# A seven-product FFN: the four weight sums of a column pair moved from GpSimd arithmetic to accumulating DMAs, and a second plain column pair ahead of the products

## The reference

```
def swiglu(x, w_gate, w_up, w_down):
    return (jax.nn.silu(x @ w_gate) * (x @ w_up)) @ w_down
...
hdn = rmsnorm(x, gains[0])
x = x + 0.5 * rmsnorm(swiglu(hdn, ffn_w_gate[layer, 0], ffn_w_up[layer, 0], ffn_w_down[layer, 0]), gains[1])
```

## Time and profile before

| | |
|---|---|
| median of 3 runs | 2672.76 us |
| the profiled execution | 2667.47 us, span 2665.7 us |
| PE busy | 2488.1 us, 93% of the span, mean granted clock 0.974 |
| DVE, ACT, POOL busy | 1749.6, 1096.3, 1009.2 us |
| seven-product phases (first to last matmul, us from the span's start) | 67 to 293, 942 to 1168, 1355 to 1581, 2283 to 2509 |
| moved by DMA | 264 MB, mean 99 GB/s |

### The profile page before, as it was taken

One profiled execution on the slowest core, in us unless ns is written; L12 is line 12 of the kernel. 1 busy time (PEld: TensorE's weight loads), 2 busy tenths in 40 slices (PEclk: granted clock), 3 DMA queues, 4 the chain that ended last, 5 costly groups with the idle time before them and its releaser, 6 DMA issues. The chain is left out here.

```text
span 2665.7 us, 50729 instructions
## 1 busy us (share of the span) xinstructions
PE 2488.1 (93%) x19573; PEld 2346.5 (88%) x19573; DVE 1749.6 (66%) x2614; ACT 1096.3 (41%) x2074; POOL 1009.2 (38%) x937
## 2 busy tenths in 40 slices
PE   5999999998999879999969999999999989699998
PEld 5899999995557879999969999999979969699998
DVE  6998525546664699862599882467546566998723
ACT  3554424114443445442445452334344444454422
POOL 3556103023331365620265630165245533656201
PEclk8999999999999989999989999999999999899999
DMA  3233432348894123343123343223210133133431
GB/s 98 80 96 96 121 85 65 80 129 286 301 306 151 48 64 96 96 120 90 29 79 96 96 124 87 64 65 88 65 34 2 33 105 92 50 95 107 112 87 45
DMA packets 315918, 264.16 MB, mean 99 GB/s; under 512 B 10984, under 2 KB 288693, under 8 KB 315688
## 3 DMA queue, kind: packets, MB, share of 16 engines
q1 hardware_dynamic: 304176, 223.03, 28.4%
q0 software_dynamic: 11536, 38.28, 4.3%
HBM read 251.71 MB, written 9.56 MB: 98 GB/s over the span
## 5 line engine op out<-in xcount | busy, mean ns | idle before, releaser
L750 PE MATMUL ps<-x_part_hi,part_hi 128*128 128x272 f32 x2240 | 660.6, 295 | 90.6 <-DVE part_lo L795 70.4
L750 PE MATMUL ps<-x_part_hi,part_lo 128*128 128x272 f32 x2240 | 654.0, 292 | 0.0
L750 PE MATMUL ps<-x_part_lo,part_hi 128*128 128x272 f32 x2240 | 650.7, 290 | 0.0
L506 DVE TENSOR_TENSOR w_lo<-w_raw,w_hi 128x1024 fp32r<-128x1024 f32 (+1 forms) x154 | 225.8, 1466 | 493.4 <-ACT w_hi L499 488.0
L750 PEld LDWEIGHTS ps<-x_part_hi,part_hi 128*128 128x128 f32 x2240 | 427.5, 191 | 103.0 <-DVE part_lo L795 72.4
L499 ACT CAST w_hi<-w_raw 128x1024 fp32r<-128x1024 f32 (+1 forms) x154 | 182.1, 1182 | 605.1 <-PE ps L534 546.0
L750 PEld LDWEIGHTS ps<-x_part_lo,part_hi 128*128 128x128 f32 x2240 | 428.5, 191 | 0.0
L750 PEld LDWEIGHTS ps<-x_part_hi,part_lo 128*128 128x128 f32 x2240 | 427.5, 191 | 0.0
L795 DVE TENSOR_TENSOR part_lo<-w_pair,part_hi 128x512 fp32r<-128x512 f32 x320 | 329.7, 1031 | 45.4 <-ACT part_hi L788 43.4
L1381 POOL TENSOR_TENSOR xT<-xT,rstd_rows 128x272 f32<-128x272 f32 x96 | 84.4, 909 | 696.5 <-DVE rstd_rows L1406 696.5
L795 DVE TENSOR_TENSOR part_lo<-w_sums,part_hi 128x512 fp32r<-128x512 f32 x240 | 260.7, 1086 | 20.0 <-ACT part_hi L788 19.3
(11 more groups left out here) (565 smaller groups left out, 5031.3 us busy)
## 6 DMA issues: line engine op xcount, KB each, us to landing
...
v_pages<-in_cache_a_v_dram POOLq DMA_DIRECT2D x128, 256.0 KB, 4.5
...
```

The source lines that it names most:

```text
L506: e.tensor_tensor(w_lo[:, n % 2, 0:nk * P], raw[:, n % RAW, 0:nk * P], w_hi[:, n % 2, 0:nk * P].bitcast(F32), ALU.subtract).then_inc(sem(" ...
L750: mm = e.matmul(ps[:, bank, 0:TH], w[:, k * P:(k + 1) * P], x[:, k, :], start=idx < 4 and k == 0 and w is wh and x is xp_hi[idx], stop=k = ...
```

## The change

The second pair of columns of gate and up is done plainly too (`STD` = 2), so that eight plain units run ahead of 18 pairs (`WP` = 18) with 126 products. The ring has four slots, not five, in four of its 26 rounds, so that 126 parts end at the same slot as 140 did.

The scheme's signs are turned so that all four sums of weights are plain sums: t3 = b12 + b22, t2 = b11 + t3, b12 + b11, t2 + b21. Some activation quarters are scaled by a negated gain (`minus_gains`) instead, and `dve_sums` subtracts where it added. Each sum is a DMA from SBUF to SBUF, issued from POOL's queue, which adds its source to its destination. A sum that may not overwrite an operand needs it twice: SP loads b12's quarter (4 x 128 rows) and b11's once more into `w_sums`. A pair is loaded by four DMAs of 512 + 256 + 512 + 256 KB, where it was two of 512 KB. The buffer's layout is now tile by tile, so that a row of a load is 512 bytes, where it was 1 KB.

POOL does no arithmetic in the gate and up phase. Its four sums of activations are DVE's, between the splits of the seventh and the eighth plain unit. For the first two pairs SP waits for the raw slots that lie under the buffer (`raw_free`).

```
-HP = KF // 2 - 1
-WP = 2 * HP
+STD = 2
+WP = 2 * (KF // 2 - STD)
 LATE = 10
+DMA_SUMS = ("t2", "t4")
...
-        w_pair = [place(f"w_pair_{x}", [P, KD, 2 * P], F32, at=at_w + x * 12288)[0] for x in range(2)]
+        w_pair = [place(f"w_pair_{x}", [P, 2, KD, P], F32, at=at_w + x * 12288)[0] for x in range(2)]
...
-                gemm(f"gate_up{l}{w}", "gate_up", 1, KD, gate_up)
+                gemm(f"gate_up{l}{w}", "gate_up", STD, KD, gate_up)
...
+        SLOTS = [(c, s) for c in range(KF + 4) for s in range(RING - short(c))]
...
-            return (w_pair[x][:, 0:KH, 0:P], part_rows(w_sums[x][:, 1, :]), w_pair[x][:, 0:KH, P:2 * P],
-                    part_rows(w_sums[x][:, 0, :]), w_pair[x][:, KH:KD, 0:P], w_pair[x][:, KH:KD, P:2 * P],
+            return (w_pair[x][:, 0, 0:KH, :], part_rows(w_sums[x][:, 1, :]), w_pair[x][:, 1, 0:KH, :],
+                    part_rows(w_sums[x][:, 0, :]), w_pair[x][:, 0, KH:KD, :], w_pair[x][:, 1, KH:KD, :],
                     part_rows(w_sums[x][:, 1, :]))[idx]
...
         def sp_gate_up(e, g, down):
             f = ffn_of(g)
             l, w = int(g["name"][-2]), int(g["name"][-1])
+            for i in range(STD):
+                for j in range(4):
+                    sp_unit(e, g, i, j)
+            of = (rows(io["ffn_w_gate"][l, w]), rows(io["ffn_w_up"][l, w]))
+
+            def raw_free(slot):
+                e.wait_ge(sem("w_lo_ready"), g["first"] + 4 * (STD - 1) + (slot - g["first"]) % RAW + 1)
+
+            for p in range(WP):
+                x, at = home(g, p), (STD + p // 2) * 2 * P
+                m1, m2 = slice(at, at + P), slice(at + P, at + 2 * P)
+                if p >= 2:
+                    wait_step(e, "vector", f, "part", PROD * (p - 1) - 1)
+                if p < 2:
+                    raw_free(2 * x + 1)
+                e.dma_start(w_pair[x][:, 1, :, :], of[p % 2][:, :, m2]).then_inc(sem(f"w_pair{p % 2}"), 16)
+                if p < 2 and x:
+                    e.wait_ge(sem("unit_done"), g["first"] + 4 * STD - 1 + (1 if g["first"] % 2 else 0))
+                e.dma_start(part_rows(w_sums[x][:, 0, :]), of[p % 2][:, 0:KH, m2]).then_inc(sem(f"w_pair{p % 2}"), 16)
+                if p < 2:
+                    raw_free(2 * x)
+                e.dma_start(w_pair[x][:, 0, :, :], of[p % 2][:, :, m1]).then_inc(sem(f"w_pair{p % 2}"), 16)
+                if p < 2 and x:
+                    e.wait_ge(sem("unit_done"), g["first"] + 4 * STD - 1 + (1 if g["first"] % 2 else 0))
+                if p < 2 and not x:
+                    raw_free(2)
+                e.dma_start(part_rows(w_sums[x][:, 1, :]), of[p % 2][:, 0:KH, m1]).then_inc(sem(f"w_pair{p % 2}"), 16)
             for j in range(4):
-                sp_unit(e, g, 0, j)
-            of = (rows(io["ffn_w_gate"][l, w]), rows(io["ffn_w_up"][l, w]))
-            for p in range(WP):
-                if p < 2:
-                    e.wait_ge(sem("w_lo_ready"), g["first"] + 4)
-                else:
-                    wait_step(e, "vector", f, "part", PROD * (p - 1) - 1)
-                at = (1 + p // 2) * 2 * P
-                for x in range(2):
-                    k = slice(x * KH, (x + 1) * KH)
-                    e.dma_start(w_pair[p % 2][:, k, :], of[p % 2][:, k, at:at + 2 * P]).then_inc(sem(f"w_pair{p % 2}"), 16)
-            for j in range(4):
-                wait_step(e, "vector", f, "part", PROD * (WP - (1 if (down["first"] + j) % RAW < 2 else 0)) - 1)
+                slot = (down["first"] + j) % RAW
+                early = slot in ((0, 1) if home(g, WP - 1) else (3,))
+                wait_step(e, "vector", f, "part", PROD * (WP - early) - 1)
                 sp_unit(e, down, 0, j)
...
+        W_LOADS = 4
+
         def pair_landed(e, f, p):
-            e.wait_ge(sem(f"w_pair{p % 2}"), 32 * ((WP * f + p) // 2 + 1))
+            e.wait_ge(sem(f"w_pair{p % 2}"), 16 * W_LOADS * ((WP * f + p) // 2 + 1))
+
+        W_ADDS = 4
+
+        def added(e, f, p, n):
+            e.wait_ge(sem(f"w_added{p % 2}"), 16 * (W_ADDS * ((WP * f + p) // 2) + n))
 
         def pool_gate_up(e, g):
             f = ffn_of(g)
-
-            for n, (to, a, b, op) in enumerate(((2, 3, 6, ALU.add), (1, 2, 0, ALU.subtract), (3, 0, 3, ALU.subtract),
-                                                (5, 4, 1, ALU.subtract))):
-                wait_step(e, "vector", f, "xn", (7, 11, 11, 15)[n])
-                if n:
-                    wait_step(e, "gpsimd", f, "x_sum", n - 1)
-                e.tensor_tensor(x_sums[:, to, :, :], x_sums[:, a, :, :], x_sums[:, b, :, :],
-                                op).then_inc(sem("ffn_gpsimd"), did("gpsimd", "x_sum", n))
             for p in range(WP):
-                x = p % 2
-                if p == 1:
-                    e.wait_ge(sem("unit_done"), g["first"] + 4)
+                x = home(g, p)
                 pair_landed(e, f, p)
-                b11, b12, b21, b22 = (w_pair[x][:, k:k + KH, m:m + P] for k in (0, KH) for m in (0, P))
+                b11, b21, b12, b22 = (w_pair[x][:, c, k:k + KH, :] for c in range(2) for k in (0, KH))
                 t3, t2 = (part_rows(w_sums[x][:, y, :]) for y in range(2))
-                e.tensor_tensor(t3, b22, b12, ALU.subtract).then_inc(sem("ffn_gpsimd"), did("gpsimd", "w_sum", 4 * p))
-                wait_step(e, "gpsimd", f, "w_sum", 4 * p)
-                e.tensor_tensor(t2, t3, b11, ALU.add).then_inc(sem("ffn_gpsimd"), did("gpsimd", "w_sum", 4 * p + 1))
-                e.tensor_tensor(b12, b12, b11, ALU.subtract).then_inc(sem("ffn_gpsimd"), did("gpsimd", "w_sum", 4 * p + 2))
-                wait_step(e, "gpsimd", f, "w_sum", 4 * p + 1)
+                e.dma_start(t3, b22, accum_op=ALU.add).then_inc(sem(f"w_added{p % 2}"), 16)
+                e.dma_start(b12, b11, accum_op=ALU.add).then_inc(sem(f"w_added{p % 2}"), 16)
+                added(e, f, p, 2)
+                e.dma_start(t2, t3, accum_op=ALU.add).then_inc(sem(f"w_added{p % 2}"), 16)
                 wait_step(e, "vector", f, "part", PROD * p + 1)
-                e.tensor_tensor(t2, b21, t2, ALU.subtract).then_inc(sem("ffn_gpsimd"), did("gpsimd", "w_sum", 4 * p + 3))
-
+                added(e, f, p, 3)
+                e.dma_start(t2, b21, accum_op=ALU.add).then_inc(sem(f"w_added{p % 2}"), 16)
...
+            if idx in (1, 2, 3, 6):
+                added(e, f, p, {1: 3, 2: 2, 3: 2, 6: 4}[idx])
...
+        X_SUMS = ((3, 0, 2, ALU.add), (2, 2, 6, ALU.add), (1, 3, 6, ALU.add), (5, 1, 4, ALU.subtract))
...
             dve_rstd_x(e, s, first + 2)
             dve_split(e, first + 3, 0, KD)
             gate(0)
-            for h, parts in ((1, (3, 6)), (0, (0, 4))):
-                for k in range(KD):
-                    e.scalar_tensor_tensor(x_sums[:, parts[k // KH], k % KH, :], xT[:, k, half(h)], gain(l, n_pre, k),
-                                           rb[:, half(h)], ALU.mult, ALU.mult
-                                           ).then_inc(sem("ffn_vector"), did("vector", "xn", (1 - h) * KD + k))
             up(0)
+            dve_split(e, first + 4, 0, KD)
+            xn(2, 1, 0, 0, plus)
+            xn(0, 0, 0, KH, plus)
             hidden(0)
             low(0)
+            dve_split(e, first + 5, 0, KD)
+            gate(1)
+            up(1)
+            xn(6, 1, KH, 2 * KH, minus)
+            xn(4, 0, KH, 3 * KH, plus)
+            hidden(1)
+            low(1)
+            dve_split(e, first + 6, 0, KD)
+            for n, (to, a, b, op) in enumerate(X_SUMS):
+                wait_step(e, "vector", f, *(("xn", 2 * KD - 1) if n < 2 else ("x_sum", (0, 2)[n - 2])))
+                e.tensor_tensor(x_sums[:, to, :, :], x_sums[:, a, :, :], x_sums[:, b, :, :],
+                                op).then_inc(sem("ffn_vector"), did("vector", "x_sum", n))
+            dve_split(e, first + 7, 0, KD)
+            gate(2)
+            up(2)
             for n in range(3):
                 dve_x_part(e, g, n)
-            gate(1)
-            for q in range(3):
-                dve_part(e, g, q)
-            for n in (3, 4):
-                dve_x_part(e, g, n)
-                dve_part(e, g, n)
+            hidden(2)
+            low(2)
+            dve_part(e, g, 0)
+            dve_part(e, g, 1)
+            gate(3)
+            dve_part(e, g, 2)
+            dve_x_part(e, g, 3)
+            dve_part(e, g, 3)
+            dve_x_part(e, g, 4)
+            dve_part(e, g, 4)
...
+            for f, (l, w) in enumerate(ffns):
+                at = (l * 6 + 4 * w) * KD + KH
+                ins = e.tensor_scalar(neg_gains[:, KH * f:KH * (f + 1)], gains[:, at:at + KH], -1.0, None, ALU.mult)
+                chain(e, ins)
```

210 lines of the change are left out of this document (122 added, 88 removed).

## The result

The changed kernel takes 2931.5 us in the median of 4 runs (2921.5 to 2935.0) against 2672.0: ratio 1.097, 95% interval 1.094 to 1.100. It is slower, as forecast, but by 260 us and not by 86, and beyond the range (2612 to 2850).

The account below looks back on a forecast made before the run. PE, 93% busy, was taken to bound the kernel. An FFN: 213.0 of matmuls + 9 start + 40 waiting for weight sums = 262 us against 240.4, +86 us over four FFNs, giving 2759 us; range 2612 to 2850.

Parts of the forecast that it names:

- Signs, gain columns: Plus for minus costs the same instruction; instructions for 24 negated gain columns ahead of everything cost at most 1 us.
- part_lo at 0.68 us: DVE's part_lo in the pairs, 0.68 to 1.78 us before, comes to 0.68; this takes away 5.8 us of small waits.
- Start, 9 us (6 to 14): Time lost at the start of each FFN's products: 9 us in place of 24.6.
- The weight sums, S = 40 us: S, an FFN's wait for load and adds: buffer loop 26.0 us against 21.0, 2.5 us a pair in 16 pairs.
- Two reads: An adding DMA fetches both operands, 0.8 us each, making the buffer loop 26.0 us, not 21.2 with one read.
- DMA share over 0.8: Sign in the profile: the DMA engines' busy share in a product phase is over 0.8.
- A phase of about 229 us: Sign in the profile: 126 products take about 229 us from product 0, for 189 us of work.
- Products wait behind part_hi for DMA: Sign in the profile: in every pair products wait behind ACT's part_hi, which waits for the DMA writing w_sums.
- Rival C: Adds' landings take 4.5 us, not 2.9: S is 78, +60 us an FFN, 2911 us in all; chance 0.08.
- Rival D: Gaps each pair send PE to 1.2 GHz: 12 us an FFN, 48 us more, 2807 us; chance 0.10.
- Rival B: Only the DMA engines' rate counts, not latencies: 11.7 us a pair, +1.6 us an FFN, 2679 us; chance 0.12.
- Rival A: Adds cost as little as copies, the loop at most 21.2 us stays behind PE: 2607 to 2631 us; chance 0.30.

Follow-up runs that it names:

- pool_sums: Changed kernel with a pair's four weight sums as POOL arithmetic and the doubled loads taken out: 2628.1 us, ratio 0.985 to the kernel before.
- no_reload: Changed kernel with only the first two pairs of each FFN loaded, later pairs adding onto the same buffers: 2699.6 us, ratio 1.011 to the kernel before.
- no_reload_reorder: Changed kernel without loads from the third pair on, and with the next pair's adds 1 and 2 issued ahead of the fourth add: 2628.7 us.
- early_half: Changed kernel with two of a pair's four loads issued after part 5 of the buffer's last pair, not part 6: 2934.5 us.
- reorder: Changed kernel with POOL issuing adds 1 and 2 of the next pair ahead of the fourth add: 2966.9 us, ratio 1.111 to the kernel before.
- filler_in_gap: Changed kernel with 24 useless matmuls that wait for nothing behind the first product of every pair but the first: 2933.6 us.
- flat: Changed kernel with add 3 reading loaded b11 in place of t3, so it needn't wait for adds 1 and 2: 2789.5 us.

## Why the prediction went wrong, step by step

- *PE bounds, and the four product phases are where it is decided*: right.
- *Added matmuls, +3.0 us an FFN*: right. *Signs, gain columns*: nothing seen. (The kernel has 16 negated columns, made by four instructions, not 24.)
- *part_lo at 0.68 us when POOL no longer reads SBUF*: right. Its median is 0.68 us in the phase, where the sums' one had 1.09. But it bought nothing, since DVE waits.
- *The gap before product 0 under 3 us*: right, 1.1, 1.1, 1.1 and 2.6.
- *Start, 9 us (6 to 14)*: wrong, 16.8. In pool_sums it is 12.0. I had written that loads, two stages of adds and a part end 5 us after product 0; it took 10.5 here, with adds and load on the same engines. +7.8 us an FFN.
- *The weight sums, S = 40 us*: this is the step that failed. Measured are 79.0 us. The error is in two sentences. "That makes 21.2 or 26.0 us" rests on a loop over one buffer with sharing of 3.2 us; the links' sizes were too low: adds 1 and 2 took 6.0 to 7.0 us, not 5.0; add 3 6.8, not 3.7; the load 9.4 in the mean from first issue to last landing, not 7.6. Only the fourth add, alone on the engines, was as forecast (3.3 for 3.7). And "POOL's queue is in order, but behind the waiting fourth add stand only the next pair's adds, whose turn comes about 1 us later" put aside the very chain that binds. With my sizes it would have been 0.5 + 5.0 + 3.7 + 1.4 = 10.6 us a pair and harmless; with the real ones it is 15.3. POOL's waits, no_reload with no_reload_reorder, and early_half show that it binds and that the loop over the buffer doesn't.
- *What each of the two errors cost*, as an estimate: with the sizes measured, written down ahead of reorder, my own loop is 28.6 us, 14.3 a pair, and S = 3.8 x 16 = 61 us. So of the 2.3 us that a pair took beyond the forecast's 13.0, some 1.3 are the sizes and some 1.0 the queue. The mechanism, landings in a row, was right; the landings beside other transfers were too short and one path was dismissed.
- Sum: 7.8 + 39.0 = 46.8 us an FFN, 187 in all. 2754 + 187 = 2941, and the profiled execution took 2934.8. The terms account for the miss to 6 us, of which 4 are that I took the second FFN's 240.4 us before for all four; their mean is 241.5.
- *Two reads*: right (2.15 times a MB; 187 ns against 84 for packets of 2 KB). *DMA share over 0.8*: wrong, 0.74, as the chain leaves the engines idle. *A phase of about 229 us*: wrong, 285 in the second FFN. *Products wait behind part_hi for DMA*: right.
- *Rival C, slow landings, 2911 us*: nearest in time, given 0.08. It took the landing of 4.5 us from the earlier trace rows; adds here land in 4.3, 5.3, 6.8 and 3.3, 4.9 in the mean. Its reason against ("adds come at most two at once") forgot that a load runs beside them. Yet it was hung on the loop over the buffer, which isn't the chain that bound, and it had every landing alike where they run from 3.3 to 6.8. That it comes within 20 us is in part luck.
- *Rival D, the clock*: its sign in the trace came true (0.89), its price didn't (filler_in_gap: none). It couldn't have been added to a chain of DMAs that PE doesn't hold up.
- *Rival B* (rate alone, 11.7 us a pair): falls by flat. *Rival A*, adds as cheap as copies: they cost twice as much, and with plain copies in their place the period was still 12.3.

What stays open: how the time would come out if POOL's queue were no chain and the loop over one buffer kept all its links. The estimate is 14.3 us a pair; reorder ties the two together, and flat, where the loop was seen to bind, has a link less. Open too is why an add beside a load takes twice its time: with two thirds of the load it still took 5.8 us.
